# A hybrid decoder layer on one core: quartered cross query weights, token turns among the memory value products, a bias read in final order, pooled channels ahead

## The reference, cut to what matters

```
z = rms(x) @ w_in                       # [q | k | v | u]; q, k, v: 12 heads of 64, u: 1280 channels
attn = dilated window attention(q, k, v) + relative bias; samples read 2048 cached keys and values
pooled = causal means over 2/4/8/16 positions of u, minus u, then a map per group
x += concat(attn, pooled) @ w_out
mk, mv = rms(mem) @ w_ck, rms(mem) @ w_cv        # 256 memory tokens, 4 heads of 128
x += cross attention(rms(x) @ w_cq, mk, mv) @ w_co
x += mixture of 32 experts(rms(x))      # top 2 of 8 in the best of 4 groups
```

## Time and profile before

| | us |
|---|---|
| median of 3 runs | 1558.89 (1555.63 to 1563.12) |
| profiled execution, span | 1559.4 |
| PE busy in it | 1255.1 |
| DVE busy | 501.4 |
| ACT busy | 194.3 |
| POOL busy | 59.6 |

### The profile page before, as it was taken

How to read it: one execution, slowest core, us unless ns; L and a number is a source line. 1 busy time by engine, 2 the same in 40 slices (tenths; PEclk the granted TensorE clock), 3 DMA queues, 4 the chain that set the end, 5 groups by cost and what they waited for, 6 DMA issues and landing times.

```text
span 1559.4 us, 23594 instructions
## 1 busy us (share of the span) xinstructions
PE 1255.1 (80%) x10109; PEld 654.8 (42%) x10109; DVE 501.4 (32%) x1042; ACT 194.3 (12%) x465; POOL 59.6 (4%) x111
## 2 busy tenths in 40 slices
PE   7999999998998998786776776776767777776776
PEld 4444467766876765332222222222222222222222
DVE  2301155740103224333323323323323322332333
ACT  3200113321111234010000000000000000000000
POOL 2000021221000000000000000000000000000000
PEclk9999999999998999898998998998998998999898
DMA  9999989999999897799999999999999999999996
GB/s 356 318 370 358 361 311 391 345 332 391 389 395 355 288 412 287 329 403 424 428 426 424 428 425 426 427 426 425 428 428 423 426 428 424 428 426 425 426 427 277
DMA packets 114030, 608.85 MB, mean 390 GB/s; under 512 B 11198, under 2 KB 14421, under 8 KB 79785
## 3 DMA queue, kind: packets, MB, share of 16 engines
q1 hardware_dynamic: 72027, 479.04, 74.6%
q10 hardware_dynamic: 34550, 100.80, 17.5%
q0 software_dynamic: 7408, 28.37, 5.1%
HBM read 603.16 MB, written 106.18 MB: 455 GB/s over the span
## 4 chain that ended last, share of the span: by engine, by line
DMA 53%; PE 42%; DVE 2%; issue 1%; SPq 1%; ACT 1%; ACTq 0%; DVEq 0%
DMA ring<-in_w_e_up_dram 46%; PE pb L1142 10%; PE pb L654 9%; PE pb L899 6%; PE pb L740 4%; DMA ring<-in_w_out_dram 2%; DMA ring<-in_w_in_dram 2%; DMA ring<-in_w_cq_dram 2%; PE pb L917 2%; PE pb L1026 2%; PE pb L682 2%; PE pb L660 1%; SPq L489 1%; DMA Z<-in_mem_prompt_dram 1%; PE pb L1006 0%
## 5 line engine op out<-in xcount | busy, mean ns | idle before, releaser
L1142 PE MATMUL pb<-ring,xT 128*32 128x256 f32 x4096 | 313.1, 472 | 196.6 <-DMA ring<-in_w_e_up_dram 189.2
L1142 PEld LDWEIGHTS pb<-ring,xT 128*32 128x32 f32 x4096 | 154.5, 134 | 378.2 <-DMA ring<-in_w_e_up_dram 238.7
L2017 DVE TENSOR_TENSOR Z<-pb,Z 128x512 f32<-128x512 f32 x248 | 153.6, 680 | 341.1 <-PE pb L1097 341.1
L654 PE MATMUL pb<-ring,hreg 128*128 128x512 f32 (+1 forms) x320 | 125.3, 551 | 0.0
L1172 PE MATMUL pb<-ring,xT 128*32 128x512 f32 x960 | 109.2, 595 | 0.0
L1097 PE MATMUL pb<-xT 32*128 32x512 f32 x744 | 102.9, 623 | 0.0
L1073 PE MATMUL pb<-Z,xT 128*32 128x512 f32 (+1 forms) x768 | 94.9, 608 | 1.0 <-DVE xT L1995 1.0
L654 PEld LDWEIGHTS pb<-ring,hreg 128*128 128x128 f32 x320 | 60.3, 190 | 61.8 <-issue 60.2
L899 PE MATMUL pb<-hreg,ring 128*128 128x264 f32 x320 | 77.7, 400 | 4.1 <-DMA ring<-in_w_out_dram 4.1
L740 PE MATMUL pb<-hreg,ring 128*128 128x264 f32 x320 | 75.3, 395 | 3.3 <-DMA ring<-in_w_in_dram 3.3
L1511 ACT ACTIVATE xT<-pb 128x128 f32<-128x128 f32 x32 | 8.9, 277 | 525.4 <-PE pb L1142 525.4
(11 more groups left out here) (333 smaller groups left out, 1142.8 us busy)
## 6 DMA issues: line engine op xcount, KB each, us to landing
ring<-in_w_e_gate_dram SPq DMA_DIRECT2D x63, 2048.0 KB, 19.0
ring<-in_w_e_up_dram SPq DMA_DIRECT2D x63, 2048.0 KB, 23.5
ring<-in_w_e_down_dram SPq DMA_DIRECT2D x30, 4096.0 KB, 22.1
out_win_k_sample_dram<-in_cache_win_k_dram ACTq DMA_DIRECT2D x24, 1536.0 KB, 13.8
out_win_v_sample_dram<-in_cache_win_v_dram ACTq DMA_DIRECT2D x24, 1536.0 KB, 13.8
ring<-in_w_in_dram SPq DMA_DIRECT2D x7, 4096.0 KB, 23.6
ring<-in_w_out_dram SPq DMA_DIRECT2D x4, 4096.0 KB, 34.4
out_win_k_sample_dram<-in_cache_win_k_dram ACTq DMA_DIRECT2D x8, 1488.0 KB, 15.4
```

The source lines that it names most:

```text
L654: last = mm(bk[:, 0:n], xt[:, k, tile * P:tile * P + P], w[:, k, 0:n], start=(k == 0), stop=(k == KT - 1))
L1142: last = mm(pb[1][32 * c:32 * c + 32, 0:256], XT[:, k % 4, 32 * (k // 4):32 * (k // 4) + 32], w[:, :, k8, P * c:P * c + P], start=(k == 0) ...
L2017: last = V.tensor_tensor(d, banks[c][:, :], d, ALU.add)
```

## The change

Five things are altered:

1. CQ is loaded as four DMAs of 1 MB with a semaphore each. DVE scales quarter j behind output tile 12+j, and PE's first cross query waits for a quarter only when it comes to it.
2. The token turns stand among the products of the first memory value tile, one group behind each of its 16 products; bias and scale products stand ahead of them. Both value tiles now go to DVE.
3. The bias rows are stored with the sign changed and 32 times over. They are read back, behind piece IN0+1 in SP's list, by four DMAs of 32 partitions each, straight into `bias` in final order. The six reversing products, their six copies and the constant `flip` go.
4. Channel block 9 stands directly behind block 8, ahead of `channel_rows(5, 8)`.
5. The product `sel` stands within the first output tile, before its last attention block.

```diff
-           + ["u", "val"] + ["turn"] * 2 + ["u", "uout", "val"] + ["sturn"] * 2 + ["u", "uout"] + ["map"] * UT + ["sel"]
+           + ["u", "val"] + ["turn"] * 2 + ["u", "u", "uout", "val"] + ["sturn"] * 2 + ["uout"] + ["map"] * UT + ["sel"]
...
-                sp.dma_start(dst, src).then_inc(w_landed[i % 2], 16)
+                if i == CQ:
+                    for j in range(4):
+                        sp.dma_start(dst[:, 4 * j:4 * j + 4], src[:, 4 * j:4 * j + 4]).then_inc(cq_landed[j], 16)
+                else:
+                    sp.dma_start(dst, src).then_inc(w_landed[i % 2], 16)
...
-            sp.dma_start(bias_dram[:, :], brow[0:H, :]).then_inc(brow_stored, 16)
+            sp.dma_start(bias_dram[:, :, :], brow[0:H, :].unsqueeze(1).to_broadcast([H, REPS, 384])).then_inc(brow_stored, 16)
+            big(IN0 + 1)
             sp.wait_ge(brow_stored, 16)
-            sp.wait_ge(v_freed, v_at("bias", 1))
-            sp.dma_start(hankel.rearrange("p (h j) -> p h j", h=H),
-                         bass.AP(tensor=bias_dram.tensor, offset=0, ap=[[1, P], [384, H], [1, SEQ]]))\
-                .then_inc(bias_landed, 16)
-            big(IN0 + 1)
+            for r in range(0, P, REPS):
+                sp.dma_start(bias[r:r + REPS],
+                             bass.AP(tensor=bias_dram.tensor, offset=P - 1 - r, ap=[[384 - 1, REPS], [384 * REPS, H], [1, SEQ]]))\
+                    .then_inc(bias_landed, 16)
...
             piece_landed(pe, CV)
-            project(hmT, wk(CV), 0, abank("cv"), a_filled)
+            cv0 = vbank("cv")
+            for k in range(KT):
+                last = mm(cv0[:, :], hmT[:, k, 0:P], wk(CV)[:, k, :], start=(k == 0), stop=(k == KT - 1))
+                if k == KT - 1:
+                    last.then_inc(v_filled, 1)
+                bk = abank("x")
+                for t in range(2):
+                    turn(bk[:, P * t:P * t + P], xraw[:, t, P * k:P * k + P], ident[:])
+                turn(bk[:, SEQ:TOK], xraw[0:NB, 2, P * k:P * k + P], ident[0:NB, 0:NB]).then_inc(a_filled, 1)
             project(hmT, wk(CV), 1, vbank("cv"), v_filled)
...
-                if n == 1:
-                    pe.wait_ge(bias_landed, 16)
-                    for f in range(6):
-                        mm(vbank("flip")[:, :], flip, hankel[:, 512 * f:512 * f + 512], start=True, stop=True)\
-                            .then_inc(v_filled, 1)
...
             channels(8)
+            channels(9)
             channel_rows(5, 8)
...
             last.then_inc(v_filled, 1)
-            channels(9)
...
+                    if o == 0 and k == KT - 1:
+                        choose_heads()
...
-            pe.wait_ge(wq_scaled, 4)
...
+                    if h == 0 and k % 4 == 0:
+                        pe.wait_ge(wq_scaled, k // 4 + 1)
...
-                if o in (KT - 3, KT - 2):
-                    piece_landed(dve, CQ)
-                    for k in range(8 * (o - KT + 3), 8 * (o - KT + 3) + 8, 4):
-                        w = wk(CQ)[:, k:k + 4, :]
-                        TT(w, w, gT[:, 2 * KT + k:2 * KT + k + 4].unsqueeze(2).to_broadcast([P, 4, 512]), ALU.mult).then_inc(wq_scaled, 1)
+                if o >= KT - 4:
+                    k = 4 * (o - KT + 4)
+                    dve.wait_ge(cq_landed[o - KT + 4], 16)
+                    w = wk(CQ)[:, k:k + 4, :]
+                    TT(w, w, gT[:, 2 * KT + k:2 * KT + k + 4].unsqueeze(2).to_broadcast([P, 4, 512]), ALU.mult).then_inc(wq_scaled, 1)
```

More of the change, by code:

```diff
@@ L43 @@
 NBUCKET, MAXD = 32, 2048
+REPS = 32
 BRANCHES = ((128, 1), (512, 4), (2048, 16))
@@ L84 @@
 NCORR = sum(n for _, _, n in CORR)
-CONST_W = dict(ident=P, tri=P, moe=NE + NE + 3 + OVB + BLK, corr=NCORR, pools=PG * NB, flip=P, hmask=VC, sel=VG * NB,
+CONST_W = dict(ident=P, tri=P, moe=NE + NE + 3 + OVB + BLK, corr=NCORR, pools=PG * NB, hmask=VC, sel=VG * NB,
                ohp=384, ohs=NDEC)
@@ L104, in constants @@
     part("ident")[:] = np.eye(P)
-    part("flip")[:] = np.eye(P)[::-1]
     part("tri")[:] = np.triu(np.ones((P, P)), 1)
@@ L312, in hybrid_decoder_layer @@
         w_landed = [sem("w_landed0"), sem("w_landed1")]
+        cq_landed = [sem(f"cq_landed{i}") for i in range(4)]
         v_filled, v_freed = sem("v_filled"), sem("v_freed")
@@ L370, in piece_landed @@
         def piece_landed(eng, i):
-            assert i != CK
+            assert i not in (CK, CQ)
             eng.wait_ge(w_landed[i % 2], 16 * (i // 2 + i % 2))
@@ L378, in a_at @@
             return nth(A_ORDER, name, j)
-        N_FIRST, N_CONST = 6, 18
+        N_FIRST, N_CONST = 6, 17
         SQ_OUT, SQ_CQ, SQ_CO = 10, 10 + KT, 14 + KT
@@ L386, in piece_used @@
             if i in (CK, CV):
-                eng.wait_ge(v_filled, v_at(("ck", "cv")[i]))
+                eng.wait_ge(v_filled, v_at("ck") if i == CK else v_at("cv", 1))
             elif i < IN0 + 4:
@@ L686, in _ @@
             memory_keys(1, vbank("ck"), v_filled)
-            for t in range(3):
-                pe.wait_ge(x_landed[t], 16)
-            for k in range(KT):
-                bk = abank("x")
-                for t in range(2):
-                    turn(bk[:, P * t:P * t + P], xraw[:, t, P * k:P * k + P], ident[:])
-                turn(bk[:, SEQ:TOK], xraw[0:NB, 2, P * k:P * k + P], ident[0:NB, 0:NB]).then_inc(a_filled, 1)
             pe.wait_ge(const_landed, 16 * N_CONST)
@@ L706, in _ @@
             last.then_inc(v_filled, 1)
+            for t in range(3):
+                pe.wait_ge(x_landed[t], 16)
             piece_landed(pe, CV)
-            project(hmT, wk(CV), 0, abank("cv"), a_filled)
+            cv0 = vbank("cv")
[7 more added lines that the diff above has]
+                turn(bk[:, SEQ:TOK], xraw[0:NB, 2, P * k:P * k + P], ident[0:NB, 0:NB]).then_inc(a_filled, 1)
             project(hmT, wk(CV), 1, vbank("cv"), v_filled)
@@ L882, in _, with choose_heads @@
             assert kt == UT
-            pe.wait_ge(v_freed, v_at("svals"))
-            bk = abank("sel")
-            for i in range(2):
-                last = mm(bk[:, 24 * i:24 * i + 24], masked[0:96, P * i:P * i + P], sel[0:96, :], start=True, stop=True)
-            last.then_inc(a_filled, 1)
+            def choose_heads():
+                pe.wait_ge(v_freed, v_at("svals"))
+                bk = abank("sel")
+                for i in range(2):
+                    last = mm(bk[:, 24 * i:24 * i + 24], masked[0:96, P * i:P * i + P], sel[0:96, :], start=True, stop=True)
+                last.then_inc(a_filled, 1)
             for o in range(KT):
@@ L1620, in _ @@
             dve.wait_ge(const_landed, 16 * N_CONST)
-            freed(V.tensor_copy(brow[0:H, :], filled("bias")[0:H, 0:384]))
+            freed(V.tensor_scalar(brow[0:H, :], filled("bias")[0:H, 0:384], -1.0, None, ALU.mult))
             freed(V.tensor_scalar(biasS, filled("bias")[:, 0:NDEC], -1.0, None, ALU.mult))
@@ L1630, in _ @@
                 head_norm(mk, t, P, XH, XD, msq, gck, mk_normed)
-            freed(V.tensor_scalar(mv[:, 1, :], filled("cv")[:, :], st[:, 22:23], None, ALU.mult))
+            for t in range(2):
+                freed(V.tensor_scalar(mv[:, t, :], filled("cv")[:, :], st[:, 21 + t:22 + t], None, ALU.mult))
             dve.wait_ge(v_freed, nv)
-            dve.wait_ge(a_freed, a_at("cv"))
             dve.nop().then_inc(mk_normed, 1)
@@ L1646, in sample_scores @@
                                 AX.X, ALU.add).then_inc(keys_used, 1)
-            for n in range(2):
+            for n in range(3):
                 project(n)
-            for f in range(6):
-                freed(V.tensor_scalar(bias_flat[:, 512 * f:512 * f + 512], filled("flip")[:, :], -1.0, None, ALU.mult))
-            project(2)
             dve.wait_ge(v_freed, nv)
@@ L1709, in _ @@
             dve.wait_ge(keys_stored, 16)
+            dve.wait_ge(bias_landed, 16 * (P // REPS))
             dve.wait_ge(a_freed, a_at("qk", 5))
```

13 lines of the change are left out of this document (4 added, 9 removed).

## The result

The changed kernel took **1570.4 us** (median of 7 runs, 1565.8 to 1573.6) against 1558.9 for the kernel before in the same session (7 runs): ratio 1.0070, 95% interval 1.0052 to 1.0087. It is slower by 0.7%, some 11 us, where 19 us less were forecast. The profiled execution's span is 1568.6, 9.2 over that of before.

A forecast was written before the change was run, and what follows sets the result against it. It took the wait for expert weights, gated by PE's front up to about 635 us, as the bound. Terms -6.8-5.2+0+2.7-9.8 = -19.1 gave 1540 us; own range 1535 to 1545, wider range 1531 to 1550.

The forecast's parts named there:

- The bias in final order: Front: six reversing products leave PE's chain, -5.2 us; the moved reads cost 0, at the other end 10 us.
- Token turns: Front, memory values: turns among the value products at 0.30 us a group, PE done at 77.9; -6.8 us, bounds -7.6 and 0.
- The thin cover: Memory keys in the front: DVE has them normed at 77.5, only 0.4 us ahead of PE, which would otherwise wait.
- The next weights: `w_in` pieces in the front: they still land in time and the wait for IN0+5 stays; 0, with 3 us either way.
- Block 9 ahead: Sample values and output tile 0: later pooling delays values 5.4 us, WOUT is no longer waited for; +2.7 us, bounds -4.2, +6.5.
- Cross queries: First cross queries: PE's wait of 7.06 us for the fourth scaled quarter and the slow run behind it go; -9.8 us.
- The slower one: Rival, front: every one of IN0+1 to IN0+4 becomes late, four times 5.7 us and a slow start of 1.8; 1570, chance 0.04.
- Weights stay where they are: Rival, front: loads, not PE, set the pace, so two gains return as a longer wait for IN0+5; 1552, chance 0.08.
- theory W: From the experiments, not the prediction: transfers bind in the front, so PE's saved time returns as waits; 1535 to 1548 without twelve copies.
- Late pooling is covered: Rival, sample values: DVE is ready sooner or block 9 is worth its 4.2 us; 1533, chance 0.10.
- Quarters land together: Rival, cross queries: all quarters land at 494.4, PE loses 4 us in query 0; 1545 to 1547, chance 0.09.

The follow-up runs named there:

- reads_early: The changed kernel with the four bias reads ahead of IN0+1 in SP's list instead of behind it; 1554.8 us, ratio 0.9974 against the kernel before.
- bias_undone: The changed kernel with the bias part taken back (single read, six reversing products and their evictions), the other four parts kept; 1560.3 us, ratio 1.0004.
- block9_alone: The kernel before with channel block 9 right behind block 8 and `sel` inside output tile 0, nothing else; 1564.1 us, ratio 1.0041.
- quarters_alone: The kernel before with the cross query weights (CQ) loaded in four quarters and nothing else; 1550.0 us, ratio 0.9955.
- between_no_turns: The changed kernel with bias reads ahead of IN0+1, row turns between blocks 8 and 9, token turns back ahead of the bias products; 1547.4 us, ratio 0.9942.

## Why the prediction was wrong

The parts, measured alone or by undoing them, add up to the whole: turns +0.05%, block 9 +0.41%, quarters -0.45%, the bias in final order -0.30% with its reads in a free queue, and +0.96% for where its reads stand (1.0070 against 0.9974). Their sum is +0.67%; +0.70% was measured. The two bias figures are themselves differences between the changed kernel, reads_early and bias_undone, so what the sum tests is the other three: +0.01% together, against +0.04% for bias_undone. From -19 forecast to +11 measured are 30 us, and the bias part has half of them.

- **The bias in final order** (forecast -5.2; came out at about +10) holds the step that failed: "I take 0 for all of it; the other end is 10 us, if SP stood that long and IN0+2 became late". SP stood that long, 30 us on the reads, and IN0+2 became late. The prediction priced the reads by their landing, 10.1 us in a queue of their own, and never priced their issue behind IN0+1, though rows of before had such prices: 6.38 and 10.48 us. The bound was also too small: 18.8 us of waiting and 3.1 of slow clock, because IN0+2 went out 5 us late and also had the reads and both stores ahead of it. Some of that came back at channel block 2, where the wait of 3.30 and its slow restart are gone. The six products themselves were worth about what was said.
- **Token turns** (-6.8; came out at 0): the failed step is "because ACT's copies pace it". PE's own turns did: a group takes 8.3/16 = 0.52 ahead of the products, where PE has no wait for ACT's copies of 0.50, and 0.56 among them, where ACT has 1.43 for a copy. The price of 0.30 came from eight turns in a row; the earlier trace rows had the two larger turns of one group at 0.38. With 16 times 0.56 in place of 4.8, and the bias and scale products at 2.4, the trace's gain is the 2.3 seen. The rest was a clock that the one profile showed low and half of the others did not. The thin cover held: DVE's last norm ended at 82.07, 0.4 ahead of PE, as forecast to the tenth, though 4.6 later.
- **The next weights** (0, 3 either way) can't be told apart from the reads in the changed kernel. With the reads ahead, PE waited 1.3, 1.6 and 0.8 for IN0+1, IN0+2 and IN0+5 and 5.5 for IN0+6, the last piece, in the profiled execution; with twelve copies less such waits went, for 4.7 us in all.
- **Block 9 ahead** (+2.7; +6.4 alone, interval +3.6 to +9.4): the mechanism and its 5.4 us were right, down to the 5.31 of the trace, and tile 0 ended 2.7 us later in block9_alone, as forecast. Some of that is luck: the slow restart cost 4.3 us, not 2.3, and 2.9 of waiting for value rows went, not 1.0. What failed is "so I count no new wait": the memory keys, WOUT+1 and WOUT+2 were waited for, and the loss was 6.4 by the end of tile 11. The bound of +6.5 held it.
- **Cross queries** (-9.8; -7.0 alone, interval -9.7 to -4.4): the mechanism was right. In quarters_alone's trace so is the size, 14.4 us for the two queries where it was 24.4; why the ratio gives less than that is not shown. The trace of after gives its loss there: the last quarter's scaling began at 517.19 and held PE 1.9 us, and the restart ran at a mean granted clock of 0.86 (519 to 531 us). By the rule that the prediction took from the Trainium skill ("DMA: Bandwidth & Descriptors", Anatomy of one DMA, a section on DMAs that POOL, there GpSimd, issues; SP issues these) the quarters would cost 6 us more in all, an estimate. From the first quarter's issue to the last landing they took 37.6 us in the changed kernel (479.58 to 517.16) and 34.2 in quarters_alone (458.09 to 492.24), against 32.5 for the whole piece: 5.1 and 1.7 more, beside other transfers, so the runs neither bear the 6 us out nor rule it out. The reading of CK's quarters in the prediction counted from the last one's own issue, which cannot show such a loss.
- **The rivals.** The slower one gave 1570, and 1570 it was, but that the numbers agree is luck: its four late loads are one load, IN0+2, 22 us dear. Its sentence named the cause ("the bias reads beside IN0+1"), and 0.04 was too little for something that rows of before spoke for. *Weights stay where they are* fell with theory W, *Late pooling is covered* with the 5.31 us, and *Quarters land together* with scalings 7.7 us apart.

What is not settled: why SP is held behind a 4 MB load; what decides whether the clock falls during the early turns; and why IN0+2 landed in 23 us in the first profile and in 24 to 35 in those that issued it on time with all copies in place.

## What to carry to other kernels

Price a moved or split DMA twice: by its landing, and by the time that its issue holds the queue's engine at the new place, which here was 0.5 us with nothing large ahead and up to 19 behind a load of 4 MB; then ask which entry of that queue is due next. Before work is moved to serve as cover, look at what it already covers where it stands: block 9 hid the pooling, and only the row turns had to stay ahead of it. And an engine is said to wait for another only when there are gaps between its own instructions; a slow stretch of the clock that one profile shows is looked for in a second before it is counted as a gain.

## What the runs showed of the hardware

What an issue cost SP went with what was ahead of it in the queue: 2.15 us for four reads at 68 us, 15.54 for the first of them right behind IN0+1, 15.24 for a store of 512 KB in its place, 11.52 for one read of 1.5 MB begun 7 us later, with 18.10 for the store after that. It also went with how fast the load ahead moved. The same store right behind IN0+1 took 6.38 us where IN0+1 landed in 23.6 (before), 12.28 at 31.1 (quarters_alone), 15.24 at 33.4 (reads_early) and 18.61 at 37.5 (between_no_turns): each time SP was free some 16 to 18 us before the load had landed.

The same instructions of PE ran at 1.2 or at 2.4 GHz around 53 us, behind 8 us of token turns, from one kernel's profile to the next, and the begin of `w_in` moved by about 3.8 us.

Taking twelve copies of 1.5 MB out of a stretch in which the transfer engines were busy at 0.95 and more of their time gained 4.7 us of some 47 that 18.9 MB take at 400 GB/s: a share near 1 did not make the transfer engines the bound here.
